# Attention values on half-chunk queries, with one masked triangle, and the output weights' maximum moved

## What is computed

```
dist = WINDOW + j - c                       # query j of a block, key c of [earlier block, own block]
mask = (dist >= 0) & (dist < WINDOW) & (key_pos >= 0)
s = einsum(q, k) * HEAD_DIM ** -0.5 + bias;  s = where(mask, s, -inf)
p = exp(s - m)                               # m: row maximum, with the sink
o = einsum(p / denom, v)
```

## Time and profile before

| | |
|---|---|
| three runs | 2040.88 us median (2040.24 to 2044.18) |
| the profiled execution | 2042.47 us, its span 2040.6 us |
| granted clock of TensorE, mean | 0.984 of full speed |
| TensorE busy | 1973.6 us, 97% of the span |
| VectorE busy | 1675.8 us, 82% |
| ScalarE busy | 876.2 us, 43% |
| GpSimd busy | 310.3 us, 15% |

### The profile page before, as it was taken

How to read it: one execution, slowest core, us unless ns; L and a number is a source line. 1 busy time by engine, 2 the same in 40 slices (tenths; PEclk the granted TensorE clock), 3 DMA queues, 4 the chain that set the end, 5 groups by cost and what they waited for, 6 DMA issues and landing times.

```text
span 2040.6 us, 36527 instructions
## 1 busy us (share of the span) xinstructions
PE 1973.6 (97%) x12910; PEld 1098.6 (54%) x12910; DVE 1675.8 (82%) x4034; ACT 876.2 (43%) x2246; POOL 310.3 (15%) x288
## 2 busy tenths in 40 slices
PE   6899999999999999989988999999999999999998
PEld 3555555555555555435455555555555555554453
DVE  7788888888888889655566888888888888897766
ACT  7744444444444446221264444444444444452100
POOL 2011111111111111030010111111111111111200
PEclk9999999999999999999999999999999999999999
DMA  9222222222222224976632222222222222458442
GB/s 333 48 42 55 60 49 49 49 64 55 49 49 49 62 55 134 215 223 155 192 122 60 50 50 54 65 49 49 49 54 60 51 59 49 107 144 192 135 132 96
DMA packets 303428, 184.17 MB, mean 90 GB/s; under 512 B 267847, under 2 KB 277000, under 8 KB 303180
## 3 DMA queue, kind: packets, MB, share of 16 engines
q1 hardware_dynamic: 287348, 151.41, 29.9%
q0 software_dynamic: 7424, 29.43, 4.0%
q10 hardware_dynamic: 8568, 2.18, 0.5%
HBM read 85.29 MB, written 41.06 MB: 62 GB/s over the span
## 4 chain that ended last, share of the span: by engine, by line
PE 83%; DVE 11%; issue 2%; ACT 2%; DMA 2%; POOL 0%; SPq 0%; DVEq 0%; ACTq 0%
PE J L588 52%; PE J L1327 13%; PE W L1026 2%; PE W L1015 2%; PE W L1100 2%; DVE W L579 1%; PE W L1130 1%; PE W L1118 1%; PE W L1089 1%; PE T L1109 1%; PE J L1064 1%; DMA ST<-ST 1%; PE W L1033 1%; PE T L1074 1%; PE W L1102 1%
## 5 line engine op out<-in xcount | busy, mean ns | idle before, releaser
L588 PE MATMUL J<-W,uT_mix 128*128 128x512 f16 (+2 forms) x3072 | 611.2, 356 | 2.7 <-issue 2.4
L588 PE MATMUL J<-W,x_mix 128*128 128x512 f16 (+2 forms) x3072 | 608.7, 355 | 2.8 <-issue 2.8
L588 PEld LDWEIGHTS J<-W,uT_mix 128*128 128x128 f16 x3072 | 298.0, 99 | 273.7 <-issue 11.8
L588 PEld LDWEIGHTS J<-W,x_mix 128*128 128x128 f16 x3072 | 297.4, 99 | 272.0 <-issue 8.9
L1443 ACT ACTIVATE PB<-J,out_scale 128x512 f32<-128x512 f32 (+2 forms) x224 | 132.9, 593 | 287.2 <-PE J L588 279.1
L1327 PE MATMUL J<-W,EM_qkR_mix 128*128 128x512 f16 x480 | 115.4, 379 | 0.0
L2366 POOL TENSOR_TENSOR ST<-HH,ge 128x512 f32<-128x512 f32 x32 | 41.4, 1293 | 408.7 <-DVE HH L1852 408.7
L2375 POOL TENSOR_TENSOR ST<-ST,ge 128x512 f32<-128x512 f32 x32 | 67.8, 2120 | 215.9 <-DVE ST L1897 215.9
L1327 PE MATMUL J<-W,x_mix 128*128 128x512 f16 x400 | 100.5, 392 | 0.0
L1407 ACT ACTIVATE sc_xr<-sc_xr,small 128x128 f32<-128x128 f32 x256 | 98.5, 386 | 0.0
L1327 PE MATMUL J<-W,uT_mix 128*128 128x512 f16 x400 | 97.7, 383 | 0.0
(11 more groups left out here) (470 smaller groups left out, 3489.2 us busy)
## 6 DMA issues: line engine op xcount, KB each, us to landing
W<-in_w_in POOLq DMA_DIRECT2D x8, 2048.0 KB, 10.9
mix_d<-ST SPq DMA_DIRECT2D x32, 512.0 KB, 2.6
sc_xr<-in_x_prompt SPq DMA_DIRECT2D x20, 512.0 KB, 4.1
sc_xr<-x SPq DMA_DIRECT2D x20, 512.0 KB, 3.8
ST<-in_w_in POOLq DMA_DIRECT2D x4, 2048.0 KB, 12.2
W<-in_w_out SPq DMA_DIRECT2D x4, 2048.0 KB, 8.2
PB<-in_x_prompt SPq DMA_DIRECT2D x6, 512.0 KB, 3.7
x<-PB SPq DMA_DIRECT2D x6, 512.0 KB, 3.5
```

The source lines that it names most:

```text
L588: mm = nc.tensor.matmul(out, stationary(k, a), moving[:, k, b, :], start=(k == 0 and n == 0), stop=(k == KT - 1 and n == 2))
```

## The change

The probabilities are not parted any more by two full masks. The 128 queries are taken in two halves c of 64, each with a PSUM bank of its own (B[0] and T[0], 256 columns). The merged rows of all 128 key places are multiplied with one set of values for each half: for the first query half the own chunk's values in key places 0 to 63 and the earlier chunk's in 64 to 127, for the second query half the own chunk's everywhere. What is wrong in the 64 key places with the queries' own numbers is put right by a term on these 64 keys: the difference of the two chunks' values (dv16) times the strictly earlier triangle of the probabilities (pT_tri). A "past_t" of 64 columns replaces the two masks. The values' slot of the earlier chunk takes the first 64 rows of the new chunk after the difference has been formed (`v_diff` on VectorE, `v_change_hi` on ScalarE, `v_change_lo` on VectorE). The order of the output weights' maximum in the last unit is changed too, and two small tiles move into a shared one (wtop, gabs). The output is the same computation.

```
         v16 = sb("v16", [P, 2, 2, P], F16)
+        dv16 = sb("dv16", [P, 2, P], F16)
-        pT_past, pT_cur = (ST[:, 1024 * i:1024 * i + 1024].bitcast(F16)...
+        pT_tri = ST[:, 0:512].bitcast(F16).rearrange("p (s h c) -> p s h c", s=2, h=A_HEADS)
+        pT = ST[:, 1024:2048].bitcast(F16).rearrange("p (s h c) -> p s h c", s=2, h=A_HEADS)
+        v_change = WR_nu_kt_xr1[:, 512:640]
+        oT_banks = [B[0], T[0]]
 # TensorE
             def values(n, attn, odd):
-                pe.wait_ge(E["pT_ready"], n)
-                terms = [(s, a, b) for s in range(1 if attn == "first" else 0, 2) for a, b in ((0, 0), (0, 1), (1, 0))]
-                for i, (s, a, b) in enumerate(terms):
-                    v, p = v16[:, 1 - odd if s else odd], pT_cur if s else pT_past
-                    for kv in range(A_KV):
-                        mm = MM(B[0][half(kv), :], v[:, a, HD * kv:HD * kv + HD], p[:, b, 4 * kv:4 * kv + 4, :],
-                                start=(i == 0), stop=(i == len(terms) - 1))
+                pe.wait_ge(E["v_steps"], keep(pe, 4 * n))
+                pe.wait_ge(E["pT_loaded"], keep(pe, 16 * n))
+                terms = ((0, 0), (0, 1), (1, 0))
+                for i, (a, b) in enumerate(terms):
+                    if i == 2:
+                        pe.wait_ge(E["pT_ready"], n)
+                    for c in range(2):
+                        v = v16[:, 1 - odd if c else odd]
+                        for kv in range(A_KV):
+                            MM(oT_banks[c][half(kv), 0:256], v[:, a, HD * kv:HD * kv + HD],
+                               pT[:, b, 4 * kv:4 * kv + 4, half(c)], start=(i == 0), stop=False)
+                for i, (a, b) in enumerate(terms):
+                    for c in range(2):
+                        for kv in range(A_KV):
+                            mm = MM(oT_banks[c][half(kv), 0:256], dv16[half(c), a, HD * kv:HD * kv + HD],
+                                    pT_tri[half(c), b, 4 * kv:4 * kv + 4, :], start=False, stop=(i == 2))
 # TensorE, unit
                 project_block(n, "akv", odd)
+                pe.wait_ge(E["em_masked"], n + 1)
                 values(n, attn, odd)
                 m_out(n)
-                if not more:
-                    top_turn(pe, layer, W_OUT)
                 pe.wait_ge(E["em_masked"], n + 1)
                 r_turn(n, T[1])
                 turn_back(n)
                 if not more:
+                    top_turn(pe, layer, W_OUT)
+                project_block(n, "aq", odd)
+                if not more:
                     top_spread(pe, layer, W_OUT)
-                project_block(n, "aq", odd)
                 r_scores(n)
 # ScalarE
             def values_back(n):
-                af(qTA_part[:], B[0], ACT.Copy, scale=v_scale[:, 1:2]).then_inc(E["oT_ready"], 1)
+                for c in range(2):
+                    op = af(oTA[:, :, 64 * c:64 * c + 64], oT_banks[c][:, 0:256].rearrange("p (t q) -> p t q", t=4),
+                            ACT.Copy, scale=v_scale[:, 1:2])
+            def v_change_hi(n, odd):
+                act.wait_ge(E["v_steps"], 4 * n + 3)
+                af(v16[0:64, 1 - odd, 0, :], PB[0:64, AV:AV + P], ACT.Copy, scale=v_scale[0:64, 0:1])
+                af(dv16[:, 0], v_change, ACT.Copy, scale=-1.0).then_inc(E["v_hi"], 1)
 # ScalarE, unit
                 if more:
                     next_hi(n)
                     evac(n, "aq")
+                    v_change_hi(n, odd)
                     mix_hi(n)
                     gate_first(n, "r")
                 else:
                     gate_first(n, "r")
+                    evac(n, "aq")
+                    v_change_hi(n, odd)
                     act.wait_ge(E["m_out_psum"], n + 1)
-                    w_out_hi(act, layer, range(0, 3))
-                    evac(n, "aq")
-                    w_out_hi(act, layer, range(3, KT))
+                    w_out_hi(act, layer, range(0, KT))
 # VectorE
             def part_probs(n):
                 dve.wait_ge(E["pT_loaded"], 16 * n)
-                for s in range(1 if attn == "first" else 0, 2):
-                    kept = const("cur_t" if s else "past_t").bitcast(F16).unsqueeze(1).to_broadcast([P, 2 * A_HEADS, P])
-                    op = V.tensor_tensor(pT_both[s], pT_both[1], kept, ALU.mult)
+                for c in range(2):
+                    rows = half(c)
+                    past = const("past_t").bitcast(F16)[rows].unsqueeze(1).to_broadcast([64, 2 * A_HEADS, 64])
+                    op = V.tensor_tensor(pT_tri[rows].rearrange("p s h c -> p (s h) c"),
+                                         pT[rows, :, :, rows].rearrange("p s h c -> p (s h) c"), past, ALU.mult)
+            def v_diff(n, odd):
+                dve.wait_ge(E["h_ready"], n + 1)
+                V.scalar_tensor_tensor(v_change, PB[:, AV:AV + P], v_scale[:, 0:1], v16[:, 1 - odd, 0, :],
+                                       ALU.mult, ALU.subtract).then_inc(E["v_steps"], 1)
+                dve.wait_ge(E["v_steps"], 4 * n + 2)
+                V.tensor_tensor(v_change, v_change, v16[:, 1 - odd, 1, :], ALU.subtract).then_inc(E["v_steps"], 1)
+            def v_change_lo(n, odd):
+                dve.wait_ge(E["v_hi"], 2 * n + 2)
+                V.scalar_tensor_tensor(v16[0:64, 1 - odd, 1, :], PB[0:64, AV:AV + P], v_scale[0:64, 0:1],
+                                       v16[0:64, odd, 0, :], ALU.mult, ALU.subtract)
+                V.scalar_tensor_tensor(dv16[:, 1], v_change, -1.0, dv16[:, 0], ALU.mult, ALU.subtract
+                                       ).then_inc(E["v_steps"], 1)
 # VectorE, unit
                 gate_cap(n, "r")
-                r_keys(n)
                 if more:
+                    r_keys(n)
                     ...
                 else:
                     ...
                     V.tensor_reduce(wo_max, wo_tops, AX.X, ALU.max).then_inc(wo_max_ready, 1)
-                    top_of_all(dve, layer, W_OUT)
                 m_result(n)
                 values(n)
                 if more:
                     next_lo(dve, n + 1)
                 else:
-                    w_out_scale(dve, layer)
+                    top_of_all(dve, layer, W_OUT)
+                    r_keys(n)
                 dve.wait_ge(E["mixmr_ready"], n)
                 m_gated(n)
                 v_lo(n, odd)
+                v_diff(n, odd)
                 if more:
                     q_lo(n, NBLK * n + 7)
+                    v_change_lo(n, odd)
                     mix_size(n, keep(dve, c - 1))
                     r_weights(n)
                 gate_inverse(n, "r")
                 if not more:
-                    w_out_lo(dve, layer, range(0, 3))
                     q_lo(n, NBLK * n + 7)
-                    w_out_lo(dve, layer, range(3, 4))
+                    v_change_lo(n, odd)
+                    w_out_scale(dve, layer)
+                    w_out_lo(dve, layer, range(0, 4))
                     r_weights(n)
                     w_out_lo(dve, layer, range(4, KT))
```

More of the change, by code:

```diff
@@ L85 @@
                      ("mask_s", 64), ("dmat_s", 256), ("inter_s", 4), ("tail_s", 4), ("full_s", 2),
-                     ("own", 8), ("one", 1), ("slot3", 256), ("past", 128), ("cur_t", 64), ("past_t", 64)])
+                     ("own", 8), ("one", 1), ("slot3", 256), ("past", 128), ("past_t", 32)])
 C4, N4 = layout([("parity", 128), ("pair", 2), ("slot", 4), ("ones", 128), ("keep", 64), ("drop", 64),
@@ L135, in shape_constants @@
     put("past", i[None, :] > i[:, None])
-    now = i[:, None] <= i[None, :]
-    for name, on in (("cur_t", now), ("past_t", ~now)):
-        put(name, on.astype(np.float16).view(f))
+    put("past_t", (i[:, None] % 64 > i[None, 0:64]).astype(np.float16).view(f))
     put("own", np.arange(TS)[:, None] // DEC_SEQ == np.arange(DEC_BATCH)[None])
@@ L285, in build @@
         gtop = sb("gtop", [P, 1])
-        wtop = sb("wtop", [P, NBLK])
+        wtop = small_p[:, 104:104 + NBLK]
         top_one = sb("top_one", [1, 1])
         wm = sb("wm", [P, 3])
-        gabs = sb("gabs", [P, KT])
+        gabs = small_p[:, 120:120 + KT]
         gs = sb("gs", [P, NBLK, KT])
@@ L620, in build @@
                  "uT_psum", "uT_hi", "uT_ready",
-                 "q_lo", "k_lo", "qT_loaded", "kT_loaded", "v_hi",
+                 "q_lo", "v_steps", "qT_loaded", "kT_loaded", "v_hi",
                  "scores_psum", "scores_read", "max_ready", "probs_ready", "p_ready", "pT_loaded", "pT_ready",
@@ L780, in turn_probs @@
         def turn_probs(sp):
-            sp.dma_start_transpose(pT_cur.rearrange("p s h c -> p (s h) c"), p_rows.rearrange("p s h c -> p (s h c)")
+            sp.dma_start_transpose(pT.rearrange("p s h c -> p (s h) c"), p_rows.rearrange("p s h c -> p (s h c)")
                                    ).then_inc(E["pT_loaded"], 16)
@@ L842, in prompt_sp @@
                 if p == 6:
-                    sp.wait_ge(E["k_lo"], N0 + 1)
+                    sp.wait_ge(E["v_steps"], 4 * N0 + 1)
                     turn_keys(sp, 0)
```

(27 more changed lines are left out.)

6 lines of the change are left out of this document (2 added, 4 removed).

## The result

The changed kernel takes 2077.64 us (median of 4 runs, 2075.58 to 2078.90) against 2041.63 us (4 runs, 2040.24 to 2044.18): ratio 1.0171, 95% interval 1.0154 to 1.0187, 36 us slower. The forecast was 2043.5 with a range to 2051. The profiled execution of the changed kernel has a span of 2073.8 us, 33.2 more than the one of before.

A forecast was written before the change was run, and what follows sets the result against it. TensorE set the pace at 46.84 us a chunk; after the change VectorE with GpSimd would hold it there. On the median 2040.88, 0.9 - 0.4 - 1.7 + 3.8 = +2.6 gave 2043.5 us, range 2038.5 to 2051.

The forecast's parts named there:

- The values block: TensorE, each chunk: six pairs and twelve quarter matmuls, four at once, take 1.2 us against 1.42, 0.2 saved.
- The masking products: VectorE, each chunk: the two smaller products take 1.4 us instead of 2.35, 0.9 saved.
- The insertion: VectorE, in front of mix_size: v_diff, v_change_lo and a wait for ScalarE add 1.25 us a chunk.
- Rival C: VectorE's additional chain exceeds the 0.9 given back plus a reserve of 0.4: slower, for example 2050 us; chance 0.22.
- The loop: The 26 equal chunks of both layers: -0.04 us each, together -1 us.
- the circle with GpSimd: L1823, GpSimd's two products, mix_lo, scores, probabilities, back to L1823: holds the chunk at 46.84 +-0.1 us, stopping the gain.
- rival B: TensorE keeps the pace because GpSimd and mix_lo miss each other: chunk 46.6, time 2037 to 2040 us; chance 0.2.
- First chunks: Each layer's first chunk: values +0.9 us for two layers, TensorE running ahead -0.35 in each.
- The last chunk: Each layer's last chunk: the late maximum makes TensorE wait 3.6 us before r_out, at 19.0 to 19.4; sum +3.8.
- The clock term: Last chunk: the wait before r_out lowers TensorE's clock to 0.50, costing 0.9 us a layer, from 0 to 1.7.
- The working of 12.1: Last chunk: steps from the query block to the weights' scale, ready 12.1 us after the values' start at the earliest.
- VectorE's part in a chunk: VectorE, each chunk: 0.9 us saved on masking, 1.25 added before mix_size, so L1823 comes 0.35 to 0.45 later.

The follow-up runs named there:

- the run without fetching: The changed kernel with 92 idle instructions hidden behind VectorE's weight differences of the first layer: 2045.86 us, ratio 1.0015 to the kernel before.
- the move alone: The kernel before with only the move of the output weights' maximum, without the values' change: 2046.95 us, ratio 1.0018.
- the run with the new last chunk: The changed kernel with 92 hidden idle instructions and, in each layer's last chunk, the output weights' scale made earlier: 2041.18 us, ratio 0.9990 to the kernel before.

## Why the forecast was wrong, step by step

Its sum left out what decides. For the rest it can be held against the run without fetching, +2.4 us measured for +2.6 forecast, but that agreement is partly luck: of the terms below some came out larger and some smaller.

**The values block** 1.2 us forecast, 1.23 measured, quarters together. **The masking products** 1.4, measured 1.38:

```profile
326.64 1.38 DVE L1910 TENSOR_TENSOR ST<-ST,k 64x1024 f16<-64x1024 f16 x2
...
340.80 0.34 DVE L2074 SCALAR_TENSOR_TENSOR WR_nu_kt_xr<-PB,v_scale,v 128x128 f32<-128x128 f32 x1
...
341.38 0.75 DVE L2090 SCALAR_TENSOR_TENSOR PB<-J,PB 128x256 f16<-128x256 f32 x2
342.14 0.34 DVE L2081 SCALAR_TENSOR_TENSOR v<-PB,v_scale,v 64x128 f16<-64x128 f32 x1
...
342.61 1.20 DVE L1930 TENSOR_REDUCE small<-ST 128x1 f32<-128x1024 f32 x1
```

**The insertion** of 1.25: 0.58 for v_diff (340.80 to 341.38) and 0.47 for v_change_lo (342.14 to 342.61), 1.05; the wait of 0.15 for ScalarE did not come. L1823's successor starts 16.15 us after the values (346.70 - 330.55) where it was 15.60 (340.91 - 325.31): 0.55 later, 0.35 to 0.45 forecast. **Rival C** needed an insertion of 1.3 and had no part in it.

**The loop.** The 26 equal chunks were forecast at -1.0 us (the other 0.7 of the -1.7 was for the first chunks). In the run without fetching the thirteen distances of each layer add up to 608.25 and 608.07 us, before 608.97 and 609.02: -1.7. The signs of the circle with GpSimd show. VectorE takes the retention result without a wait, and mix_lo starts inside GpSimd's end and takes 1.60 instead of 1.28 us:

```profile
391.32 0.42 DVE L1854 TENSOR_TENSOR HH<-W,k 128x256 f32<-128x256 f32 x1
...
392.50 1.60 DVE L1943 SCALAR_TENSOR_TENSOR ST<-ST,small 128x1024 f16<-128x1024 f32 x1
...
392.30 0.72 POOL L2442 TENSOR_TENSOR ge<-ge,head_g 128x256 f32<-128x256 f32 x1
```

But this circle did not stop the gain, as the forecast had it. Where VectorE's late row work reaches TensorE, the copy on ScalarE stood behind the row exponentials for nothing. With it ahead the chunk is TensorE's 46.66, rival B's figure, though GpSimd's products and mix_lo stand where they stood, and VectorE again waits about 0.1 us for TensorE in front of the retention result. The 46.8 was right, the cause given for it was not.

**First chunks** +0.45 each for the values block, less 0.35 each for TensorE running ahead, so +0.1. Measured without fetching 0.8 and 0.6 (47.0 and 46.8 us for 46.2): the running ahead did not show, and it is a little more than the values block's own 0.5.

**The last chunk.** r_out at 19.0 to 19.4 behind the values, with a wait of 3.6: measured 831.17 - 811.81 = 19.36 and 3.69, against the earlier trace rows. The clock term was too small. The granted clock was 0.50, 1.2 GHz, from 831.4 to 838.1, twice as long as in the earlier trace rows (the same columns):

```profile
831.17 1.86 PE L1140 MATMUL W<-PB,WR_nu_kt_xr 128*128 128x64 f32 x8 [3.69 <-DVE WR_nu_kt_xr L2096]
```

```profile
831.40:838.10 6.70, 6.70 (x27) 3.58 (x27) 6.64 (x9) 3.80 (x5) 0.00 (x0) 0.50 0.49 95
1848.60:1851.90 3.30, 3.30 (x17) 1.80 (x17) 3.28 (x4) 2.79 (x3) 0.00 (x0) 0.50 0.14 33
```

I had taken 0.9 us a layer. Half of 6.7 and of 3.3 is 3.4 and 1.7, and from r_out to the chunk's end it took 3.3 and 1.6 us longer than before. With r_out itself 0.3 and 1.9 later the chunks grew by 3.7 and 3.5 us, 7.2 in all for +3.8. (The working of 12.1 has two slips that cancel: its steps add up to 11.9, and what the 8.2 leave is 6.5, not 6.3.)

In the time, the move alone cost +3.5 all the same. Part of the growth comes back behind the chunk: the stretch from there to layer 1's first values stage was 290.2 us after and 297.7 before, and 290.0 in the run without fetching. The clock was at its lower level for 23.9 us of it after and 30.7 before, which makes 3.4 of the 7.5; what makes the rest no run shows. In the trace of the run without fetching the first chunks (+1.4), the equal chunks (-1.7) and the last chunks (+7.9) make +7.7, and this stretch takes 7.8 back. The forecast held neither the 7.9 nor the 7.8.

**The step that failed** is the one named "VectorE's part in a chunk". It costed the four added operations, and the waits with them, as durations, and asked which chain they lengthen; what they add to the length of VectorE's program it put at nothing without a word. The change makes the loop's turn nine instructions longer (332 to 341) and puts eight more ahead of the first. In layer 0 the loop's end stood at remainder 48, 7 to 17 records in front of the edge, and was moved to 65; in layer 1 it went from 32 to 74. The 10 waits of 3.0 us, in a kernel whose reserve of 0.68 us the same change had just used up, are 30 of the 36 us. No rival held it: C had the right sign (slower, above 46.95) for another reason. What pointed to it was in the data of before: q14 with 35 packets on the page, and none of them in the loops in the trace.

## What to carry to other kernels

In a kernel with a loop on the device, the number of VectorE's instructions in a turn and ahead of it is a cost term of its own (for the other engines no run here shows one): compare the packets on the instruction queues, and look for an idle time put down to "issue" at the first operation behind the branch. Here it jumped by 1.5% for nine instructions in the turn and eight ahead of it, and vanished with some that do nothing, so a change should not be judged before its place has been varied. Only then does the order of work speak: here the values' change was worth nothing that could be told from zero, the order of a layer's last chunk 4 to 5 us, and the move of one copy on ScalarE 3 to 6.

## What was not expected of the hardware

VectorE's instruction packets are 8 KB, four are kept as far as the runs tell, and a jump to one that is gone stops the engine for 2.5 to 3.4 us. Another queue, q8, brings packets of 16 KB, one for some 256 instructions of TensorE, so I take it to be TensorE's; none comes in the loops of either kernel, though TensorE's turn has 1,291 instructions before and 1,343 after. A pair of waits on a satisfied semaphore costs VectorE 0.10 us (9.8 us for 95), and nothing that shows behind an operation of 0.4 us (with 96 such pairs the first values stage starts at 138.65, before at 138.59).

The granted clock moves the time from execution to execution: the twelve of the changed kernel without fetching reach from 2039.45 us at a mean of 0.986 to 2052.61 at 0.979. The stretches at 1.2 GHz add up to 48 us in the trace of the run with the new last chunk (span 2030.7) and to 79 us in the changed kernel's. Two such stretches fell into the changed kernel's loop, behind the waits of TensorE at the loop's end (449 and 644 us), and their chunks took 50.5 and 50.7 instead of 49.5 to 50.0; behind the other eight waits the clock stayed at 2.4 GHz. I have no experiment on what decides it.
